# Layer 1's output projection: four tiles together and four one by one in halves of k, low parts on VectorE, first loads moved into the heads' phase

## The reference

```python
# layer 1, latent tokens only: y is the mLSTM output (1024 x 2048), already times its SiLU gate
o   = y @ o_w_out                      # 2048 x 1024
r   = ALPHA * x1 + gate * o            # ALPHA = 4 ** 0.25, gate: one row of 1024
mu  = mean(r); var = mean((r - mu)**2)
out = (r - mu) * rsqrt(var + 1e-5) * ln_g + ln_b
```

## Time and profile before

| | us |
|---|---|
| median of three runs | 2857.88 |
| the profiled execution | 2855.51 |
| its span | 2853.7 |
| heads' last store issued | 2624.82 |
| first matmul of the projection | 2637.88 |
| first group's last matmul done | 2726.6 |
| second group's last matmul done | 2785.0 |
| third group's last matmul done | 2834.6 |
| last norm done | 2848.83 |

### The profile page before, as it was taken

One profiled execution on the slowest core, in us unless ns is written; L12 is line 12 of the kernel. 1 busy time (PEld: TensorE's weight loads), 2 busy tenths in 40 slices (PEclk: granted clock), 3 DMA queues, 4 the chain that ended last, 5 costly groups with the idle time before them and its releaser, 6 DMA issues. The chain is left out here.

```text
span 2853.7 us, 50750 instructions
## 1 busy us (share of the span) xinstructions
PE 2457.5 (86%) x21262; PEld 2040.7 (72%) x21262; DVE 1691.2 (59%) x2524; ACT 935.4 (33%) x1572; POOL 707.8 (25%) x689
## 2 busy tenths in 40 slices
PE   6899999996898986787959999999599899995986
PEld 2577776775877864666848878787488788884865
DVE  3026878644356444674675566655578888876333
ACT  2112344231232323555123333333434343442311
POOL 1111110115756752000122222222211121111421
PEclk8899999998899997788979999999799999997998
DMA  7612545545233233124443444443725353422521
GB/s 275 246 53 71 156 127 160 171 142 170 79 112 100 82 94 106 27 58 155 134 85 133 154 169 149 160 170 140 251 89 172 117 172 135 153 69 86 199 92 60
DMA packets 346945, 376.11 MB, mean 132 GB/s; under 512 B 111767, under 2 KB 283550, under 8 KB 344158
## 3 DMA queue, kind: packets, MB, share of 16 engines
q1 hardware_dynamic: 337008, 365.35, 39.6%
q10 hardware_dynamic: 9710, 7.53, 0.9%
HBM read 232.96 MB, written 139.86 MB: 131 GB/s over the span
## 5 line engine op out<-in xcount | busy, mean ns | idle before, releaser
L469 PE MATMUL PS<-hT_hi,w_in_hi 128*128 128x512 f32 (+1 forms) x640 | 239.7, 375 | 4.4 <-DVE q_out L3137 4.4
L470 PE MATMUL PS<-hT_lo,w_in_hi 128*128 128x512 f32 (+1 forms) x640 | 236.4, 369 | 0.0
L471 PE MATMUL PS<-hT_hi,w_in_lo 128*128 128x512 f32 (+1 forms) x640 | 236.2, 369 | 0.0
L469 PE MATMUL PS<-h_hi,w_in_hi 128*128 128x512 f32 (+1 forms) x624 | 230.7, 370 | 5.4 <-PEq L115 3.7
L470 PE MATMUL PS<-h_lo,w_in_hi 128*128 128x512 f32 (+1 forms) x624 | 226.1, 362 | 0.0
L471 PE MATMUL PS<-h_hi,w_in_lo 128*128 128x512 f32 (+1 forms) x624 | 225.6, 362 | 0.0
L3334 PE MATMUL PS<-Q_hi,K_hi 128*128 128x256 f32 x640 | 188.5, 294 | 30.4 <-DMA K_lo<-kl_d 15.0
L3513 POOL TENSOR_TENSOR weights_lo<-weights,weights_hi 128x1280 fp32r<-128x1280 f32 x32 | 96.9, 3028 | 444.0 <-ACT weights_hi L3440 444.0
L3335 PE MATMUL PS<-Q_lo,K_hi 128*128 128x256 f32 x640 | 186.5, 291 | 0.0
L3336 PE MATMUL PS<-Q_hi,K_lo 128*128 128x256 f32 x640 | 186.1, 291 | 0.0
L3125 DVE SCALAR_TENSOR_TENSOR xnew<-padl,tile_cols,xnew 128x1024 f32<-128x1024 f32 x128 | 168.5, 1317 | 3.4
(11 more groups left out here) (464 smaller groups left out, 6258.6 us busy)
## 6 DMA issues: line engine op xcount, KB each, us to landing
chunk_in<-in_d SPq DMA_DIRECT2D x40, 512.0 KB, 3.4
w_in<-in_e_w_in_dram SPq DMA_DIRECT2D x30, 512.0 KB, 5.0
xnew<-in_o_w_in_dram SPq DMA_DIRECT2D x30, 512.0 KB, 6.4
in_d<-xnat SPq DMA_DIRECT2D x20, 640.0 KB, 6.2
modw<-in_mod_w_dram SPq DMA_DIRECT2D x12, 1024.0 KB, 9.7
xnat<-in_mod_w_dram SPq DMA_DIRECT2D x8, 1536.0 KB, 7.2
v_d<-xnew SPq DMA_DIRECT2D x16, 640.0 KB, 2.9
kh_d<-k_hi SPq DMA_DIRECT2D x16, 640.0 KB, 2.9
```

Of the source, the lines that this page charges most:

```text
L469: pe.matmul(PS[:, bank + off // 512, 0:n], wh[:, k], hh[:, k, t], start=(k == 0), stop=False)
L470: pe.matmul(PS[:, bank + off // 512, 0:n], wh[:, k], hl[:, k, t], start=False, stop=False)
L471: last = pe.matmul(PS[:, bank + off // 512, 0:n], wl[:, k], hh[:, k, t], start=False, stop=(k == KT - 1))
```

## The change

The diff replaces `out_phase` by `out1_phase` and moves loads. It does this:

- The eight tiles are taken as four together over all 16 slices, then four one by one. A single tile comes in two halves of eight slices (`load_half`, one DMA of 512 KB in rows of 512 bytes), each with one high part on ACT and one low part on POOL, in three slots. PE goes through all eight slices of a half before the next.
- In the first group both low parts are VectorE's; POOL works for the halves only. The ring of y's high and low parts has six slots instead of three, that of raw y four.
- VectorE takes and norms tile by tile: take(n), norm(n). The norm's result stays in `resid`, now a ring of three, and is stored from there; take(n) waits for the store of tile n - 3. x has two slots.
- The load of gate, norm rows and x moves from slice 3 to slice 6.
- `v_raw` and `sx_in` of the heads are allocated outside `mlstm_heads` at the right side of SBUF and live on: `v_raw` holds w, y and the gate row, `sx_in` holds x. In the last head, once `v_raw` has been split, SP loads the first two slices of w and four of y (`load_next`), ahead of stores 6 and 7. Store 7 counts on a semaphore of its own, `y_last`, which is waited for at slice 6 of the projection and not at the end of the heads' phase.

The diff's core:

```diff
-def out_phase(nc, A, G, layer, yT_d, w_out, n_k, tiles, x_of, xnew, store, extra=None):
+def out1_phase(nc, A, G, B, w_out, x_of, store):
+        held = G.vraw[:].rearrange("p a b c -> p (a b c)")
+        w = held[:, 0:2 * D].rearrange("p (a n) -> p a n", n=D)
+        y = held[:, 2 * D:4 * D].rearrange("p (a t) -> p a t", t=4 * P)
+        gate = held[:, 4 * D:5 * D]
+        x = G.sx[:].rearrange("p k t -> p (k t)").rearrange("p (a n) -> p a n", n=D)
+        yh, yl = sb("y_in_hi", [P, 6, 4 * P], F32R), sb("y_in_lo", [P, 6, 4 * P], F32R)
+        r = sb("resid", [P, 3, D])
...
+            def slot_used(eng, u):
+                if u < 3:
+                    eng.wait_ge(s["used"], 12 + 2 * u)
+                else:
+                    eng.wait_ge(s["half_used"], u - 2)
             @block.sync
+                def load_half(u):
+                    if u < 2:
+                        sp.wait_ge(s["yh_ok"], 14 + 2 * u)
+                        sp.wait_ge(s["yl_ok"], 14 + 2 * u)
+                    else:
+                        sp.wait_ge(s["th_ok"], u - 1)
+                        sp.wait_ge(s["tl_ok"], u - 1)
+                    n, k = FIRST + u // 2, HALF * (u % 2)
+                    sp.dma_start(raw_half(u), B.y_d[k:k + HALF, :, n * P:(n + 1) * P].rearrange("k p t -> p k t")).then_inc(t_in[u % 2], 16)
                 def finish(n):
                     sp.wait_ge(s["added"], n + 1)
+                    sp.dma_start(store(n), r[:, n % 3]).then_inc(stored[n % 3], 16)
+                    if n + 2 < TILES:
+                        sp.wait_ge(s["summed"], n + 1)
+                        sp.dma_start(x[:, n % 2], x_of(n + 2)).then_inc(x_in[n % 2], 16)
+                for k in range(2, NT1):
+                    sp.wait_ge(s["wh_ok"], k - 1)
+                    sp.wait_ge(s["wl_ok"], k - 1)
+                    sp.dma_start(w[:, k % 2], w_out[k * P:(k + 1) * P, :]).then_inc(w_in[k % 2], 16)
+                    if k >= 4:
+                        sp.wait_ge(s["yh_ok"], k - 3)
+                        sp.wait_ge(s["yl_ok"], k - 3)
+                        sp.dma_start(y[:, k % 4, :], B.y_d[k][:, 0:FIRST * P]).then_inc(y_in[k % 4], 16)
+                    if k == 6:
...
+                        sp.wait_ge(G.y_last, 16)
+                        for n in range(2):
+                            sp.dma_start(x[:, n], x_of(n)).then_inc(x_in[n], 16)
+                for u in range(5):
+                    load_half(u)
+                finish(0)
+                finish(1)
+                load_half(5)
+                finish(2)
+                finish(3)
+                load_half(6)
+                load_half(7)
+                for n in range(FIRST, TILES):
                     finish(n)
             @block.tensor
+                for u in range(UNITS):
+                    n = FIRST + u // 2
+                    pe.wait_ge(s["th_ok"], u + 1)
+                    pe.wait_ge(s["tl_ok"], u + 1)
+                    if u % 2 == 0:
+                        pe.wait_ge(s["taken"], n - 3)
+                    hi, lo = half(yh, u), half(yl, u)
+                    for i in range(HALF):
+                        for h in range(2):
+                            last = products(n, h, hi[:, i, :], lo[:, i, :], HALF * (u % 2) + i)
+                    last.then_inc(s["half_used"], 1)
             @block.vector
+                for k in range(NT1):
+                    dve.wait_ge(s["wh_ok"], k + 1)
+                    dve.tensor_tensor(wl[:, k], w[:, k % 2], wh[:, k].bitcast(F32), ALU.subtract).then_inc(s["wl_ok"], 1)
+                    dve.wait_ge(s["yh_ok"], k + 1)
+                    if k >= 6:
+                        dve.wait_ge(s["used"], k - 5)
+                    dve.tensor_tensor(yl[:, k % 6, :], y[:, k % 4, :], yh[:, k % 6, :].bitcast(F32), ALU.subtract).then_inc(s["yl_ok"], 1)
...
+                for n in range(TILES):
+                    take(n)
                     norm(n)
             @block.scalar
...
+                for u in range(3):
+                    high(u)
+                root(0)
+                root(1)
+                high(3)
+                root(2)
+                root(3)
+                high(4)
+                root(4)
+                high(5)
+                high(6)
+                root(5)
+                high(7)
+                root(6)
+                root(7)
             @block.gpsimd
+                for u in range(UNITS):
+                    pool.wait_ge(s["th_ok"], u + 1)
+                    slot_used(pool, u)
+                    pool.tensor_tensor(half(yl, u), raw_half(u), half(yh, u).bitcast(F32), ALU.subtract).then_inc(s["tl_ok"], 1)
 def mlstm_heads
                 def store(u):
                     sp.wait_ge(s["y_ok"], 4 * (u + 1))
-                    sp.dma_start(half_rows(B.y_d, u), sx[:]).then_inc(s["stored"], 16)
+                    sp.dma_start(half_rows(B.y_d, u), sx[:]).then_inc(s["stored"] if u + 1 < 2 * HEADS1 else G.y_last, 16)
+                def load_next():
+                    sp.wait_ge(s["v_lo"], 4 * HEADS1)
+                    held = vraw[:].rearrange("p a b c -> p (a b c)")
+                    sp.dma_start(held[:, 0:2 * D].rearrange("p (a n) -> p a n", n=D),
+                                 A.p["o_w_out"][0][0:2 * P, :].rearrange("(a p) n -> p a n", p=P)).then_inc(s["next_in"], 16)
+                    sp.dma_start(held[:, 2 * D:4 * D].rearrange("p (a t) -> p a t", t=4 * P),
+                                 B.y_d[0:4, :, 0:4 * P].rearrange("a p t -> p a t")).then_inc(s["next_in"], 16)
+                    else:
+                        load_next()
                     store(2 * h)
                     load_skip(2 * h + 1)
                 store(2 * HEADS1 - 1)
-                sp.wait_ge(s["stored"], 32 * HEADS1)
+                sp.wait_ge(s["next_in"], 32)
+                sp.wait_ge(s["stored"], 32 * HEADS1 - 16)
```

More of the change, by code:

```diff
@@ new lines, in out1_phase, with raw_half, half @@
+        TILES, FIRST = NCH - CTXCH, 4
+        HALF = NT1 // 2
+        UNITS = 2 * (TILES - FIRST)
+        def raw_half(u):
+            return y[:, 2 * (u % 2):2 * (u % 2) + 2, :].rearrange("p a (k t) -> p (a k) t", t=P)
+        def half(buf, u):
+            a = 2 * ((u + 2) % 3)
+            return buf[:, a:a + 2, :].rearrange("p a (k t) -> p (a k) t", t=P)
+        sems = ("y_in0 y_in1 y_in2 y_in3 t_in0 t_in1 w_in0 w_in1 wh_ok wl_ok yh_ok yl_ok th_ok tl_ok row_in x_in0 x_in1 used half_used "
+                "taken summed mean_ok root added stored0 stored1 stored2 step eps_ok")
@@ new lines, in products @@
+                def products(n, h, hi, lo, k):
+                    out, c = PS[:, 2 * (n % 4) + h, :], slice(512 * h, 512 * h + 512)
+                    pe.matmul(out, hi, wh[:, k, c], start=(k == 0), stop=False)
+                    pe.matmul(out, hi, wl[:, k, c], start=False, stop=False)
+                    return pe.matmul(out, lo, wh[:, k, c], start=False, stop=(k == NT1 - 1))
+                for k in range(NT1):
+                    pe.wait_ge(s["wh_ok"], k + 1)
+                    pe.wait_ge(s["wl_ok"], k + 1)
+                    pe.wait_ge(s["yh_ok"], k + 1)
+                    pe.wait_ge(s["yl_ok"], k + 1)
+                    for n in range(FIRST):
+                        t = slice(n * P, n * P + P)
+                        for h in range(2):
+                            last = products(n, h, yh[:, k % 6, t], yl[:, k % 6, t], k)
+                    last.then_inc(s["used"], 1)
@@ L3188, in mlstm_heads @@
         KH, KL = (sb(n, [P, 4, T], F32R) for n in ("K_hi", "K_lo"))
-        vraw = sb("v_raw", [P, 4, NCH, P])
+        vraw, sx = G.vraw, G.sx
         VH, VL = sb("V_hi", [P, NCH, 4 * P], F32R), sb("V_lo", [P, NCH, 4 * P], F32R)
```

194 lines of the change are left out of this document (48 added, 146 removed).

## The result

The changed kernel takes 2819.88 us (median of four, 2814.07 to 2822.63), against 2858.54 us for four runs of the kernel before on the same chip: 0.987 of it, 95% interval 0.9843 to 0.9898. Its profiled execution took 2820.11 us with a span of 2818.3 us. The forecast was 2822 us, with 2820.1 us and 2818.3 us for the profiled run and its span.

A forecast was written before the change was run, and what follows sets the result against it. TensorE, busy 86% of the span, was taken as the bound, standing still at the projection's head, two later groups and tail. -9.1 - 19.3 - 7.0 = -35.4 us from the 2857.9 median gave 2822 us, range 2811 to 2838.

The forecast's parts named there:

- The head: Heads' last store to the projection's first matmul: earlier block start and preloaded slices give -9.1 us, bounds 0 and 13.1.
- Rival A: Head gives less: block's end still awaits the store (+3.8) or preload delays heads (up to +9); 2826 to 2832, chance 0.07.
- The first group: Projection's first four tiles: same 384 matmuls, supply runs ahead, 88.7 us unchanged; cost 0, bounds 0 and +5.
- The hole at the change: Change to single tiles: PE waits 1.41 us for the first take, as before and in layer 0; difference 0.
- The tiles: Four single tiles: 384 matmuls without holes at full clock, 87.1 us plus 0.2 instead of 106.6, so -19.3 us.
- rival C: TensorE's granted clock falls in the tile stage and stays down: slower, +77 us with all 384 matmuls, 2899 us; chance 0.03.
- The tail: After the last matmul: one take and one norm, 7.2 us instead of 14.2, so -7.0 us, bounds -6 and -7.5.
- B: Tile stage: one or two halves come late behind a norm, exposing 7.3 us each; 2830 or 2837 us, chance 0.08.
- D: No measurable difference: moved v_raw and sx make the heads run 3.5% longer, 21 us; about 2844 us, chance 0.03.
- signs named in advance: Expected in the profile, among others: heads' last store at 2624.8 as before, first group 88.8 us and tiles 87.3 us.

The follow-up runs named there:

- store_wait: Changed kernel with the wait for the heads' last store put back at the end of the heads' phase: 2824.78 us, 0.9893 of the kernel before.
- load_inside: Changed kernel with the first loads of w and y made inside the projection instead of in the last head: 2825.40 us, 0.9895 of the kernel before.
- tiles_only: Changed kernel with all three head changes undone (store wait, early loads, w's low parts on VectorE), single tiles kept: 2829.68 us, 0.9925 of the kernel before.
- pool_low_w: Changed kernel with w's low parts in the first group back on GpSimd: 2826.08 us, 0.9887 of the kernel before.
- groups_44: Kernel before with the projection's tile groups 4, 4 in place of 4, 2, 2: 2847.83 us, 0.9975 of the kernel before.
- groups_41111: Kernel before with tile groups 4, 1, 1, 1, 1 in place of 4, 2, 2, still by slices: 2879.15 us, 1.01 of the kernel before.
- early_take_split_last: Changed kernel with tile 0 taken once its own matmuls end and the last half computed by column halves: 2817.51 us, 0.9877 of the kernel before.
- root_before_half: Changed kernel with ACT's third half behind three roots and one SP load behind a norm: 2825.28 us, 0.9899 of the kernel before.
- best_sp_clears: early_take_split_last with all phases' semaphores cleared by SyncE instead of GpSimd: 2826.08 us, 0.9899 of the kernel before.

## Why the prediction was right

**The head**, forecast -9.1, measured -8.98. The memset comes 0.93 us after the issue of the last store (forecast 0.82), the matmul 3.15 us after it (3.16). It had two bounds far apart, 0 and 13.1, and the inner value was read from layer 0's start, a stage that begins in this very way. store_wait and load_inside show that both of its halves were needed: 3.8 and 6.4 us. (What they cost one at a time is more than they gave together, as tiles_only shows.) Rival A is refuted in both its parts: the wait for the store went (0.93 against store_wait's 4.71 us), and the heads of load_inside, with no early loads, are no shorter where these loads would stand (436.64 against 436.73 us).

**The first group**, forecast unchanged, measured +0.95. The supply kept up: ACT's wait for w behind the lump of loads was 7.62 us instead of the earlier trace rows's 9.64, and PE has no idle row, as argued. What came in addition is the clock. The first matmuls last 0.63 us, the granted clock at its lower level of 1.2 GHz, in both kernels; 6 of them before, 11 after, and 5 x 0.2 us is the 1 us. Counted as rows of 0.6 us or more, the number was 10 in store_wait, 13 in load_inside, 12 in pool_low_w, 6 in groups_44 and 14 in groups_41111, whose PE had stood idle for 11.08, 13.63, 10.37, 16.44 and 16.55 us (7.30 after, 16.28 before). It doesn't follow the length of the idle time, as the last two show best, and what sets it stays open.

**The hole at the change**, 1.41 us as read in layer 0 and before, and early_take_split_last shows that it is the wait for take(0), which needed only tile 0's matmuls.

**The tiles**, forecast -19.3, measured -19.28, the term that mattered most. Taking layer 0's rate (283 matmuls in 64.20 us) for 384 matmuls gave 87.3 us, and 87.33 were measured. Three things in its argument were tested. That a norm in front of a supply in a hand-written queue makes the holes: groups_41111 makes them worse, groups_44 takes them away, both by how many matmuls stand behind one place in the queue. The order on ACT by itself isn't shown, since root_before_half made no hole. That VectorE's collisions with GpSimd cost up to 2.4 us without harm: a residual step took 3.41 instead of 1.23 us beside a POOL operation of 2.40, with PE full. (They did shift the queues: root(1) came 13.5 us after the first group's end and not 11.5, and high(3) right behind it.) And that the clock stays up: 1.00, so that rival C, at +77 us, didn't happen. The Trainium skill (TensorE: Matmul & The Clock Gate, section "A second HAM failure mode: psum-queue depth-cycling") was named for C; four pairs of banks in turn with one idle time of 1.41 us kept a clock of 1.00 here, so this trace doesn't show what that section describes. groups_41111 does show a clock that falls with idle times, 0.68 over 32 us with 48 matmuls in them.

**The tail**, forecast -7.0, measured -6.94, and the last store +0.34, not forecast.

**The rivals.** B, halves that come late, didn't happen, and even the three norms in front of a half in root_before_half made no hole, though only by some 0.6 us. D, heads that get longer by the new place of their buffers, looks at first as if it had half come true: 167.33 instead of 164.27 us to their first store. But groups_44 and groups_41111, with the heads of the kernel before, take 167.21 and 167.63 us, and tiles_only, with the buffers in their new place, 164.10. (The 165.06 us of best_sp_clears begin at a load that comes 2.4 us late; with these they are 167.5.) So the stretch takes 164.1 to 164.3 us in two of the profiles and 167.2 to 167.7 us in the others, whatever the kernel, and the profile of before is one of the two. What decides between them stays open.

**What was luck.** The span came out to the tenth because errors cancelled: -4.80 and +3.06 ahead of the change, +0.26, +0.95 and +0.34 behind, in all -0.2 us. The -4.80 belongs to no part of the change: layer 0's memset, 700 us ahead of the heads, already came at 1327.23 instead of 1332.33, and the profiles of all kernels here have it between 1320.77 and 1332.62. Without it the same reasons would have given a number some 5 us off, still inside the range. Two of the signs named in advance failed, by this scatter and by the clock: the heads' last store came at 2623.34 and not 2624.8, and the first group took 89.70 us and not 88.8.

## What to carry to other kernels

Where an order written out by hand puts a norm (or any wait on another engine) between two supplies of TensorE, compare its length with the matmuls that one supply carries: 1.36 us of them per slice gave 137.6 us, 2.72 gave 108.0, and 5.5 or 10.9 us gave the full stage's 88.7, with the same arithmetic and norms of 6.2 us or more (the case of 10.9 us has a new order in the queues as well). Make the supply longer before reordering the queue, and make the group that is finished last small, since its norms have nothing to lie beside. A stage of the same kernel that already has the new shape is worth more than any estimate: three of the forecast's terms were read from layer 0's, and all came within 0.2 us.

## What the runs showed of the hardware

- GpSimd clears the semaphores of a block that has ended one by one, 0.07 us each in pool_low_w; with 54 of them its first work came 3.78 us after the memset, and 1.23 us after it when SyncE cleared them. An engine whose first operation is wanted at once in a new block pays for it.
- A load of 512 KB that was issued 0.8 us behind the issue of a store took 6.52 us to ACT's start, against 4.25 us for the load of the earlier trace rows.
- The granted clock stood at its lower level for the first 6 to 14 matmuls of the projection, with no order by the idle time in front of them (7.3 to 16.6 us; 6 after 16.44 us, 14 after 16.55 us).
- Holes cost more than their idle time: in groups_41111 32.0 us of idle rows went with 64 matmuls of some 0.63 instead of 0.39 us, and the stage was 48.9 us longer.
- Two stretches ahead of the change vary from profile to profile without any change of the code in them: the time to layer 0's memset by 12 us, and the heads' first 164 to 168 us. From profile to profile they make most of the difference in the time to the heads' last store (2616.73 to 2628.62 us).
